# Sparse attention scores from halves and rests in three one-pass products, with the residual kept in DRAM during attention

## The reference

```python
q_rot = rope_partial(q, pos)            # 8 heads of 64
ks = rope_partial(ks, pos)              # 2 kv heads, selected branch
kw = rope_partial(kw, pos)              # 2 kv heads, window branch
...
s = jnp.einsum('bcgrd,bgcnd->bcgrn', qrb, k_g) * scale     # selected branch
...
s = jnp.einsum('bcgrd,bngd->bcgrn', qrb, kb) * scale       # window branch
...
x = layer_norm(ALPHA * x + (1.0 + g1) * mix, ln1_g[l], ln1_b[l])
```

## Time and profile before

| what | value |
|---|---|
| median of 3 runs | 1642.72 us (1642.53 to 1643.39) |
| the profiled execution | 1642.32 us, span 1640.5 us |
| PE busy | 1610.1 us, 98% |
| DVE busy | 998.2 us, 61% |
| ACT busy | 626.5 us, 38% |
| fp32 sparse scores, L1832 | 47.4 us in 192 records |
| bytes moved | 193.07 MB, mean 118 GB/s |

### The profile page before, as it was taken

The page is one execution under the profiler, slowest core; times in us unless marked ns, Lnnn a source line. Parts: engine busy times, 40 slices in busy tenths (PEclk is TensorE's granted clock), DMA queues, the critical chain, the costliest instruction groups (busy, mean ns, idle before and its releaser), DMA issues.

```text
span 1640.5 us, 21315 instructions
## 1 busy us (share of the span) xinstructions
PE 1610.1 (98%) x8402; PEld 1273.6 (78%) x8402; DVE 998.2 (61%) x1534; ACT 626.5 (38%) x1121; POOL 78.1 (5%) x134
## 2 busy tenths in 40 slices
PE   7999999999999999999999999999999999999996
PEld 3878776678878888888878877777887888888885
DVE  4776787868785555546676757776668433333444
ACT  2432455454263322222254335455535433232221
POOL 2300000000001011000010000000000000000000
PEclk9999999999999999999999999999999999999998
DMA  9844222235346666655436322111223333334331
GB/s 310 268 146 128 65 60 57 65 104 167 91 118 195 200 188 184 190 168 168 118 91 180 90 65 53 40 27 51 86 84 90 103 90 103 100 94 120 95 100 58
DMA packets 276818, 193.07 MB, mean 118 GB/s; under 512 B 6808, under 2 KB 263120, under 8 KB 276720
## 3 DMA queue, kind: packets, MB, share of 16 engines
q1 hardware_dynamic: 263968, 147.42, 31.0%
q0 software_dynamic: 12608, 43.77, 8.8%
q10 hardware_dynamic: 144, 0.52, 0.1%
HBM read 189.59 MB, written 2.10 MB: 117 GB/s over the span
## 4 chain that ended last, share of the span: by engine, by line
PE 93%; DVE 3%; ACT 1%; issue 1%; DMA 1%; SPq 0%; DVEq 0%; ACTq 0%
PE banks L1690 24%; PE banks L1692 23%; PE banks L1691 23%; PE banks L1863 3%; PE banks L1832 3%; PE banks L1891 2%; PE banks L1838 1%; PE banks L1767 1%; PE banks L1769 1%; PE banks L1768 1%; PE banks L1842 1%; PE banks L1897 1%; PE banks L1754 1%; PE banks L1782 1%; PE banks L1750 1%
## 5 line engine op out<-in xcount | busy, mean ns | idle before, releaser
L1690 PE MATMUL banks<-u_hi,w_hi 128*128 128x512 f32 x1112 | 455.7, 410 | 3.5 <-DVE u_lo L1270 2.0
L1049 DVE TENSOR_TENSOR w_lo<-ring,w_hi 128x1024 fp32r<-128x1024 f32 (+3 forms) x239 | 286.9, 1202 | 281.0 <-ACT w_hi L767 280.0
L1692 PE MATMUL banks<-u_hi,w_lo 128*128 128x512 f32 x1112 | 434.9, 391 | 0.0
L1691 PE MATMUL banks<-u_lo,w_hi 128*128 128x512 f32 x1112 | 434.7, 391 | 0.0
L767 ACT ACTIVATE w_hi<-ring 128x1024 fp32r<-128x1024 f32 (+2 forms) x242 | 249.9, 1033 | 160.9 <-PE banks L1692 61.7
L1690 PEld LDWEIGHTS banks<-u_hi,w_hi 128*128 128x128 f32 x1112 | 209.4, 188 | 50.2 <-issue 6.7
L1692 PEld LDWEIGHTS banks<-u_hi,w_lo 128*128 128x128 f32 x1112 | 209.0, 188 | 44.7
L1691 PEld LDWEIGHTS banks<-u_lo,w_hi 128*128 128x128 f32 x1112 | 210.0, 189 | 33.9
L937 ACT ACTIVATE probs<-banks,neg_max 128x128 f32<-128x128 f32 (+3 forms) x192 | 99.0, 524 | 150.9 <-DVE neg_max L1474 150.9
L1690 PE MATMUL banks<-h_hi,w_hi 128*128 128x512 f32 x352 | 137.9, 392 | 0.0
L1692 PE MATMUL banks<-h_hi,w_lo 128*128 128x512 f32 x352 | 137.2, 390 | 0.0
(11 more groups left out here) (281 smaller groups left out, 2232.1 us busy)
## 6 DMA issues: line engine op xcount, KB each, us to landing
ring<-in_w_ffn_in_dram SPq DMA_DIRECT2D x88, 512.0 KB, 3.9
ada_ring<-in_w_ada_dram POOLq DMA_DIRECT2D x80, 512.0 KB, 4.3
ring<-in_w_in_dram SPq DMA_DIRECT2D x72, 512.0 KB, 3.8
ring<-in_w_ffn_out_dram SPq DMA_DIRECT2D x32, 448.0 KB, 3.3
ada_first<-in_w_ada_dram SPq DMA_DIRECT2D x16, 512.0 KB, 7.5
ring<-in_w_out_dram SPq DMA_DIRECT2D x16, 512.0 KB, 3.6
ring<-in_w_ffn_out_dram SPq DMA_DIRECT2D x16, 512.0 KB, 4.0
w<-in_cmp_w_k_dram SPq DMA_DIRECT2D x8, 512.0 KB, 6.1
```

The source lines that it names most:

```text
L1049: V.tensor_tensor(lo, src, hi.bitcast(fp32), ALU.subtract).then_inc(split_lo, 1)
L1690: M(bank, wh[:, block], sh[:, k, :], start=start, stop=False)
L1691: M(bank, wh[:, block], sl[:, k, :], start=False, stop=False)
L1692: return M(bank, wl[:, block], sh[:, k, :], start=False, stop=stop)
```

## The change

The keys and queries after `rope` are split as weights are. `rope` now writes its sum in place into `raw` and signals `rope_sum`. ACT makes the rounded half, `q_hi` or `k_hi` (`high_part`; for a key branch four copies, as the other rows need it too), and DVE the rest, `q_lo` or `k_lo` (`low_part`). A sparse step makes three products per head from them. The memsets behind `rope` are gone.

The rests need 16 KB per partition, which the arena does not have. They are put where `res` lies. So ACT issues a store of `res` to a DRAM tensor `kept` before them (`keep_residual`) and a load back behind the attention loop (`fetch_residual`); DVE waits for the store ahead of the first rest and for the load ahead of `layernorm(l, 0)`. In layer 1 all eight `residual(1, m)` stand inside `keep_residual`, ahead of the store.

Declarations of semaphores are left out, and the name of `k_dup`'s view changes to `k_hi`.

```diff
@@ -148,7 +148,9 @@
 RAW = ["ksl", "kwn"] + [f"{a}{i}" for a in ("kd", "qd") for i in range(4)]
-ROPE = ["ksl", "kwn"] + [f"{a}{i}" for a in ("qn", "kd", "qd") for i in range(4)]
+ROPE = RAW[2:]
+HALVED = ["ksl", "kwn"] + [f"qn{i}" for i in range(4)]
+KEPT = [16 + 32 * l for l in range(DEPTH)]
 MERGED = 2
@@ -255,7 +257,12 @@
         w_lo = sb("w_lo", [P, NQ, SLOT], fp32r)
         ada_ring = sb("ada_ring", [P, NA, D_MODEL])
+        res_at = -(-nc.sbuf_base // 32) * 32
         res = sb("res", [P, KD, SEQ])
+        kept = nc.dram_tensor("kept", (DEPTH, P, KD, SEQ), fp32, kind="Internal").ap()
+        q_lo = nc.alloc_sbuf_tensor_at("q_lo", [P, 4, SEQ], fp32r, offset=res_at)[:, :, :]
+        k_lo = nc.alloc_sbuf_tensor_at("k_lo", [P, 4, SEQ], fp32r, offset=res_at + 4 * 4 * SEQ)[:, :, :]\
+            .rearrange("p (b g) t -> p b g t", b=2)
         arena_at = -(-nc.sbuf_base // 32) * 32
         sb("arena", [P, 62 * SEQ])
@@ -273,7 +280,8 @@
         probsT_all = at("probsT", 24, 4)
         qdT = at("qdT", 28, 4)
         kdT = at("kdT", 32, 4)
-        k_dup_all = at("k_dup", 36, 4)
+        q_hi = at("q_hi", 16, 4, fp32r)
+        k_hi_all = at("k_hi", 36, 4, fp32r)
         gm_late = at("gm_late", 36, 4)
         vd_all = at("vd_tok", 40, 4)
         v_all = at("v_tok", 44, 2)
@@ -809,9 +822,12 @@
                 if r == 0:
                     act.wait_ge(u_ready, (2 * l + 1) * KD)
-                elif r >= 2:
-                    act.wait_ge(rope_done, l * 14 + ROPE.index(RAW[r - 2]) + 1)
+                elif 2 <= r < 4:
+                    act.wait_ge(roped_low, (l + 1) * len(HALVED) + r - 3)
+                elif r >= 4:
+                    act.wait_ge(rope_done, l * len(ROPE) + ROPE.index(RAW[r - 2]) + 1)
                 wait_done(act, l, name)
                 nc.scalar.activation(raw[:, r % 2, :], bank_of(l, name), ACT.Copy, scale=scale)\
                     .then_inc(saved(l, name), 1)
@@ -862,6 +878,38 @@
                 nc.scalar.activation(res[:, m, :], res[:, m, :], ACT.Identity, bias=add_r[:, which, m:m + 1],
                                      scale=mul_r[:, which, m:m + 1]).then_inc(res_ready, 1)
+            def high_part(l, n):
+                act.wait_ge(rope_sum, l * len(HALVED) + n + 1)
+                src = raw[:, n % 2, :]
+                if n >= 2:
+                    nc.scalar.activation(q_hi[:, n - 2, :], src, ACT.Copy).then_inc(roped_high, 1)
+                    return
+                for g in range(2):
+                    own = src[64 * g:64 * g + 64, :]
+                    nc.scalar.activation(k_hi[64 * g:64 * g + 64, n, g, :], own, ACT.Copy)
+                    last = nc.scalar.activation(k_hi[64 - 64 * g:128 - 64 * g, n, g, :], own, ACT.Copy)
+                last.then_inc(roped_high, 1)
+            def keep_residual(l):
+                if l == 0:
+                    act.wait_ge(x_saved, KD)
+                    act.dma_start(kept[l], res[:, :, :]).then_inc(res_kept, 16)
+                    return
+                for half in (1, 0):
+                    part = slice(4 * half, 4 * half + 4)
+                    for m in range(4 * half, 4 * half + 4):
+                        residual(1, m)
+                    act.wait_ge(res_ready, KD + 8 - 4 * half)
+                    act.dma_start(kept[l, :, part, :], res[:, part, :]).then_inc(res_kept, 16)
+            def fetch_residual(l):
+                act.wait_ge(scored, score_step(l, LAST_NSA[-1]) + 1)
+                act.wait_ge(res_kept, KEPT[l])
+                act.dma_start(res[:, :, :], kept[l]).then_inc(res_back, 16)
             for l in range(DEPTH):
@@ -882,6 +930,9 @@
                 if l == 0:
                     prepare(0, "vsg2")
                     prepare(0, "qn0")
+                high_part(l, 0)
+                keep_residual(l)
+                high_part(l, 1)
                 for name in VSG:
                     prepare_behind(l, name)
                 for i in range(TT):
@@ -891,8 +942,8 @@
                     nc.scalar.activation(v_tok[:, i, :], token_bank(i)[:, 0:256], ACT.Copy).then_inc(v_saved, 1)
                 for i in range(4):
                     save(l, f"qn{i}", q_raw[:, i, :], HEAD_DIM ** -0.5)
-                    if l:
-                        residual(1, i)
+                    if i:
+                        high_part(l, 1 + i)
                     if i == 1:
                         act.wait_ge(v_saved, TT * (l + 1))
                         nc.scalar.activation(gates[:, :, :, :], gates[:, :, :, :], ACT.Sigmoid)\
@@ -900,18 +951,17 @@
                     elif i >= 2:
                         r = i - 2
-                        act.wait_ge(rope_done, 14 * l + r + 1)
+                        act.wait_ge(roped_low, len(HALVED) * l + r + 1)
                         for g in range(2):
-                            last = nc.scalar.activation(k_dup[64 - 64 * g:128 - 64 * g, r, g, :],
-                                                        k_dup[64 * g:64 * g + 64, r, g, :], ACT.Copy)
+                            last = nc.scalar.activation(k_lo[64 - 64 * g:128 - 64 * g, r, g, :],
+                                                        k_lo[64 * g:64 * g + 64, r, g, :].bitcast(fp32), ACT.Copy)
                         last.then_inc(k_spread, 1)
+                high_part(l, 5)
                 wait_done(act, l, "hid")
                 nc.scalar.activation(hid_tok, bank_of(l, "hid")[:, 0:CMP_HIDDEN], ACT.Gelu_apprx_tanh)\
                     .then_inc(saved(l, "hid"), 1)
                 for r, name in enumerate(RAW[2:], 2):
                     save_raw(l, name, r, HEAD_DIM ** -0.5 if name[:2] == "qd" else 1.0)
-                    if l and name[:2] == "kd":
-                        residual(1, r + 2)
                 for name in VD:
                     prepare_behind(l, name)
                 if l == 0:
@@ -961,6 +1011,7 @@
                                              nsa_ps.rearrange("p (c t) -> p c t", c=4), ACT.Copy)\
                             .then_inc(nsa_saved, 1)
+                fetch_residual(l)
                 prepare_behind(l, f"gm{GM_IN}")
                 act.wait_ge(dsq_ready, l + 1)
                 nc.scalar.activation(d_sq[:, :], d_sq[:, :], ACT.Sqrt, bias=eps[:, :],
@@ -1125,16 +1176,29 @@
                 link(V.tensor_scalar(add_r[:, to_r, :], b, ALPHA, None, ALU.mult))
                 V.memset(d_mix[:, 0:1], 0.0).then_inc(signal, 1)
-            def rope(l, r, src, outs_of):
+            def rope(src, dst, signal, count):
                 shuffle = [i + 8 if i < 8 else i - 8 if i < 16 else i for i in range(32)]
                 V.tensor_tensor(t1, src, cos, ALU.mult)
                 link(V.stream_shuffle(t2, src, shuffle))
                 link(V.tensor_tensor(t2, t2, sin, ALU.mult))
-                for dst, rows in outs_of:
-                    last = V.tensor_tensor(dst, t1[rows, :], t2[rows, :], ALU.add)
-                link(last)
-                V.memset(d_mix[:, 1:2], 0.0).then_inc(rope_done, 1)
+                V.tensor_tensor(dst, t1, t2, ALU.add).then_inc(signal, 1)
+                dve.wait_ge(signal, count)
+            def low_part(l, n):
+                dve.wait_ge(roped_high, l * len(HALVED) + n + 1)
+                src = raw[:, n % 2, :]
+                if n >= 2:
+                    last = V.tensor_tensor(q_lo[:, n - 2, :], src, q_hi[:, n - 2, :].bitcast(fp32), ALU.subtract)
+                else:
+                    if n == 0:
+                        dve.wait_ge(res_kept, KEPT[l])
+                    for g in range(2):
+                        rows = slice(64 * g, 64 * g + 64)
+                        last = V.tensor_tensor(k_lo[rows, n, g, :], src[rows, :], k_hi[rows, n, g, :].bitcast(fp32),
+                                               ALU.subtract)
+                last.then_inc(roped_low, 1)
             def layernorm(l, which):
                 n = 2 * l + which
@@ -1154,7 +1218,10 @@
                     if m >= 2:
                         link(unshift(m))
                     prepare_behind(l, names[m])
-                    if n >= 1 and m == 0:
+                    if which == 0 and m == 0:
+                        dve.wait_ge(res_back, 16 * (l + 1))
+                    elif m == 0:
                         dve.wait_ge(res_ready, n * KD)
                     wait_done(dve, l, names[m])
@@ -1346,16 +1413,16 @@
                     if l == 0 and name == "kwn":
                         prepare(0, "qn0")
                     wait_saved(dve, l, name)
-                    rope(l, r, raw[:, r % 2, :],
-                         [(k_dup[64 * g:64 * g + 64, r, g, :], slice(64 * g, 64 * g + 64)) for g in range(2)])
+                    rope(raw[:, r % 2, :], raw[:, r % 2, :], rope_sum, l * len(HALVED) + r + 1)
                 for name in VSG:
                     prepare_behind(l, name)
                 if l == 0:
                     sum_lambda()
                 for i in range(4):
```

(22 more changed lines are left out.)

7 lines of the change are left out of this document (6 added, 1 removed).

## The result

| | before | after |
|---|---|---|
| median of 20 runs each | 1642.75 us (1642.35 to 1643.53) | 1645.56 us (1644.38 to 1646.35) |
| ratio, 95% interval | | 1.0017, [1.001, 1.0023] |
| the profiled execution: own time, span | 1642.32, 1640.5 us | 1645.02, 1643.1 us |

The changed kernel is 2.8 us slower. The prediction was 1645.7 us. The page of the kernel after answers to the earlier trace rows: PE and DVE busy, the clock by slice, the chain's shares.

What follows compares the result with a forecast made beforehand. PE was taken to bound the kernel, busy 98% of the span. The terms -6.5 + 6.3 + 2.0 + 1.2 = +3.0 on 1642.32 gave 1645.3, and with 0.4 for the median 1645.7 us; the forecast's own range was 1641.5 to 1650.

Steps and rivals of the forecast that it cites:

- The products: Sparse score blocks in attention: three one-pass products replace two fp32 ones, 3.2 us gained per layer, 6.5 us in all.
- The fixed 0.21 us: Time per sparse score block beside its streamed columns, expected to stay after the change.
- the rival in which it vanishes: Sparse score blocks: the fixed 0.21 us goes with fp32's records, gain 16.6 us, time 1635.6 us; chance 0.12.
- The rival of halves that run one after the other: Sparse score blocks: one-pass halves not side by side, 11 us slower instead of 6.5 faster, 1663 us; chance 0.05.
- The prediction's figure for it: Sparse score products: by the skill's rule, each pair exposes a weight load of some 0.1 us, gain about 3 us.
- The wait before `vsg2`: Layer 1: PE stands still from 866.8 to 873.0 while ACT does copies and residuals first, 6.3 us lost, bounds 5.3 and 7.5.
- The clock: Behind PE's layer-1 gap: the clock falls and work runs at half rate, 2.0 us lost, bounds 0 and 3.5.
- the rows of the kernel's end: Trace rows at the kernel's end: the granted clock fell about 2 us after PE's work ended.
- The start-up rows: Trace rows at the beginning: 512-column products of 0.63 then 0.40 us, read as some 3 us of work at the lower clock.
- The rival in which the clock stays up: Layer-1 gap: the clock stays up and the store hides, no change, 1642.5 us; chance 0.18.
- Layer 0: Store of `res` and added DVE and ACT work in layer 0: 1.2 us lost, bounds 0 and 4.
- my bound: Layer 0: ACT's round of `qn2`, at 72.02 before, comes up to 7 us later.

Runs made afterwards that it cites:

- the order by head: Changed kernel with the six products of a sparse step reordered, three of head 0 and then three of head 1: 1645.51 us (one run).
- the first experiment: Changed kernel with the split of `vsg2` moved ahead of the first copies (`high_part(l, 0)`) in ACT's order: 1642.92 us, ratio 1.0001.
- the four places tried: Token splits behind ACT's block (changed kernel), `vsg2`'s ahead of it, `vsg2`'s before the last four copies, or all ahead: 1645.56, 1642.92, 1641.74, 1645.75 us.
- the one-product kernel: Changed kernel with only the product of `q_hi` and `k_hi` in the sparse scores, the two with the rests left out: 1632.37 us (one run).
- the three other executions with the same code: Changed kernel with sparse scores by one fp32 product per head, by three products head after head, or by one rounded product: 1650.59, 1645.51, 1632.37 us.
- the spread order: Changed kernel with ACT's layer-1 copies and residuals in groups between the splits of `vsg2`, `qn0` and `qn1`: 1638.4 us, ratio 0.9971.
- the late stores: Kernel with layer 1's groups between token splits, both its `res` stores put behind the split of `qn1` and the last four copies: 1637.49 us, ratio 0.9969.

## Why the prediction was right

**The products (predicted -6.5, measured -5.9).** Blocks were predicted at 0.89, 0.73 and 0.57 us and take 0.90, 0.73 and 0.55. The fixed 0.21 us stayed, so the rival in which it vanishes fell; the block of one product confirms it, 0.43 us being 0.21 and one product of 0.22. The rival of halves that run one after the other fell twice, in the changed kernel and with the order by head. Weight loads between products of the same rows stayed hidden: each product beyond the first adds some 0.24 us to a block of 512 columns (0.43 with one, 0.90 with three), where its pass is 0.21, and in a block that begins at 282.34 the load for the second pair begins at 282.45, while the next products start only at 282.68. The rule of the Trainium skill that a load overlaps a running product only when the row group differs ("TensorE: Matmul & The Clock Gate", The mechanism) does not agree with these rows. The prediction's figure for it, a gain of about 3 us, does not follow from its own terms either: with 0.1 us a load, one load more exposed in each of 48 blocks leaves 1.7 us, and three leave a loss of 7.9. That the 0.21 us stay fits what the Trainium skill says of a change of tiling mode ("TensorEngine Tiling (Array Packing)", Key Properties); the runs do not show whether it is the change of mode that takes them. By the blocks a layer gains 3.2 us; the traces give 2.9 and 3.0. What takes the other 0.2 to 0.3 us was not looked for.

**The wait before `vsg2` (predicted 6.3, measured 6.27).** The mechanism is the predicted one. The agreement to 0.03 us is luck: the prediction's own times, 866.8 to 873.0, are 6.2 apart, and its steps have small errors that cancel: from the first copy to the round 11.8 us instead of 12.3, as residuals in a row follow each other every 0.73 us and not 0.80, while ACT waits 0.4 us more at each store; from the round to PE's first product 1.6 us instead of 1.5. Four of the kernels have exactly this wait. What I did not see is that the block is too long to stand whole, and not only in the wrong place: the splits of `vsg2`, `qn0` and `qn1` are due 3 us and then some 5.5 us apart, the loads of the last two land only 3 to 5 us ahead of that, and none of the four places tried took the block without a wait of 3.7 us or more. I had expected the first experiment to remove the loss, and it moved the wait to `qn0`.

**The clock (predicted 2.0, bounds 0 and 3.5).** It fell as the rows of the kernel's end had suggested, though later: 1.9 us after PE's stop at the end, 3.0 us here. The start-up rows were the weaker half of the argument. They have long products at 21.94, but the profile gives a granted clock of 1.00 from 13 to 30 us, so the lower level was inferred there from the length alone; behind the gap here the clock itself reads 0.50 for 3.6 us of work. It costs 1.6 us in the profiled execution of the changed kernel and up to 2.6 in others with the same code, 2.2 on average, shown by keeping PE busy through the gap. The rival in which the clock stays up fell.

**Layer 0 (predicted 1.2, bounds 0 and 4).** This term was too large. The store did push the load of `qn2`, whose round moved from 72.02 to 77.75, near my bound; but PE's next need was later than that load by enough in most executions. In ten of twelve profiled executions of this code and its variants (two of them without the store) layer 0's projections cost -0.14 to -0.03 us; in the changed kernel's it is +0.36, in the one-product kernel's +0.44, and there PE's wait for ACT's save of `kd0` is 0.2 us longer behind the latest loads of `qn2`. Otherwise DVE's and ACT's added work is hidden, as predicted.

**What was not in the sum.** 0.7 us of the profiled difference lie ahead of any changed code. In the twelve executions this offset goes from 0.03 to 0.78, 0.42 on average, so much of it is the spread of the start-up. All twelve are above the one profiled execution of the kernel before; whether that one was early or the changed code starts a little later, one profile of it cannot tell. The offset made up for a part of the layer-0 term. That the sum met the median within 0.2 us is therefore luck in part: of the terms, the products fell short by 0.6 us, the delay and the clock together by 0.9, layer 0 by 0.8, and the start-up gave back 0.7.

Together: -5.9 + 7.4 + 0.4 + 0.7 = +2.6 us, the difference of the spans. The delay and the clock were predicted at 8.3 together and cost 7.4 there, 8.2 to 8.4 in the three other executions with the same code. A loss in one place that is larger than a gain spread over 48 blocks was nearly the whole case; in the spread order, which takes the loss out, the kernel is 4.8 us faster than before.

## What to carry to other kernels

Before work is added to an in-order queue that also feeds the bottleneck, compare the length of the added block with the room between two pieces of work that the queue already feeds: from the earliest time at which the first can be done, which its load sets, to the latest at which the second must be. Here a block of 12 us had no such room in any order tried, and pieces of 6, 3 and 3 us did. A gap of the matrix engine of 3.7 us or more cost more than its length here, since the clock fell in it or just behind it and stayed low into the work behind, so a delay of 6 us is to be priced at about 8 (7.4 to 8.4 in four executions); a gap of 1.1 us did not do it. A cut in the bottleneck's passes need not be worth its full time: one more cut of two products here was worth two thirds to three quarters of it, in part because PE then waited for DVE and ACT.

## What the runs showed of the hardware

- Two 64-row halves run side by side in both orders of the program that were tried: three products of one head followed by three of the other give the same pairs of records and the same 0.90 us as when they alternate.
- A block of 64-row products has about 0.21 us beside its columns, with one one-pass product, with three, and with fp32.
- A gap of 3.7 us was long enough to bring the clock down, 1.5 us after PE had resumed: it was at 0.50 for 3.4 us in all, by the windows. With gaps of 4.0, 6.3 and 7.1 us it was down for 6.8 us. It fell 2.2 to 5.3 us after PE's stop in these kernels and 1.9 us after it at the end of the kernel before. Of a gap of 1.1 us nothing was seen.
- A weight load for the same 64 rows began 0.11 us behind the products before it, while they ran, and three one-pass products cost 0.90 us a block.
- A DMA that ACT issues can leave ahead of the activations written before it: the late stores left at 867.88, with four copies before them in the program that ran from 868.84 on.
- Where the store ran beside the loads, the DMA moved 408 GB/s in layer 0, against 322 with the loads alone at the same full share. So the store costs the loads less than its bytes, which at 322 GB/s are 6.5 us for 2.1 MB: a load of 512 KB landed 5.6 us later in layer 0, and the split of one began 2.9 us later in layer 1.
